# Fetching and multiplying the first strip of each 64-slot unit inside the 128-slot unit ahead of it

## The chip, the core and the metric

The kernel runs on one core of a Trainium2 chip. The metric is the device time of one launch in microseconds; lower is better. The time before is the median of three runs.

## What is computed

The reference is a two-layer decoder trunk on 256 tokens of width 1024. The change lies in its last part, a layer of 8 experts of which each token uses two:

```python
def moe_swiglu(xn, w_router, we_gate, we_up, we_down):
    logits = (xn @ w_router).astype(jnp.float32)
    top_v, top_i = lax.top_k(logits, TOP_K)
    top_w = jax.nn.softmax(top_v, axis=-1)
    gates = jnp.sum(jax.nn.one_hot(top_i, N_EXPERTS, dtype=jnp.float32) * top_w[..., None], axis=-2)
    y = jnp.zeros_like(xn)
    for e in range(N_EXPERTS):
        y = y + gates[..., e:e + 1].astype(xn.dtype) * swiglu(xn, we_gate[e], we_up[e], we_down[e])
    return y
```

All weights are float32; an expert has three matrices of 1024 x 3584, 44 MB in all.

## The kernel before

The experts are ranked by how many tokens they got and worked off as eight units, in turns one of 128 slots (units 0, 2, 4, 6, called wide) and one of 64 slots (units 1, 3, 5, 7, called narrow; `NARROW_UNITS`). A unit gathers its tokens' rows, multiplies them by one expert's weights and scatters the results. Further units, for experts with more tokens than slots, run only when there are any.

**Weights.** A unit has 42 chunks of 1 MB (`FFN_CHUNKS`). They go through a ring of 9 slots in SBUF (`RING`; six of the tile `raw`, two of `spare`, one `late_slot`). SP issues one transfer per chunk in the order in which TensorE uses them (`expert`, L491): gate and up of the first strip of 1024 columns (8 chunks), then twice gate and up of a further strip and four chunks of down (12 chunks each), then a small strip of 512 columns (4 chunks) and the last six chunks of down. `place` (L288) gives the chunk's lap and slot. Before each issue `slot_free` (L427) waits until the slot's former chunk is used: for a narrow unit's chunk until TensorE has multiplied it (`piece_used`), for a wide unit's until it is split (`lo_ready`).

**Wide units** multiply in three terms of a rounded and a remainder part. ScalarE writes the rounded half chunk into `w_hi` (L1596), VectorE the remainder into `w_lo` (L2211). There are six split places of half a chunk, so the splitting runs at most three chunks ahead of TensorE. TensorE (`unit`, L1495) does gate and up of a strip with `e_in_wide`, turns the product of the strip before with `e_turn` (L1317), and multiplies it by down with `e_down`; a chunk has 12 matmuls. Near its end it turns the next unit's gathered rows (`gathered_turned`, L1280).

**Narrow units** multiply the raw chunks in float32, both halves of a chunk into the two 64-partition sides of a bank (`n_in`, `n_down`; 8 matmuls a chunk), the tokens in `x_half`. The product of a strip is a silu on ScalarE (L2067), a multiplication on VectorE (L2982), and four transposes (`n_turn`, L1409). Each engine has its order written out by hand: `narrow_unit` and `unit` on TensorE (L1431, L1495), ScalarE (L2059, L2098) and VectorE (L2975, L3013). Each has waits on counters of what the others have done.

**Rows.** GpSimd gathers the next unit's rows into `xg` (L650), once the slots of that unit are known and the former rows are turned, and scatters a unit's result when it is scaled (L655).

Of the kernel before, what the change touches and what calls it, by code (L numbers as in the profile page):

```python
# [12 lines left out]
P = 128  # L13
# [21 lines left out]
def hybrid_trunk(  # L35
# [45 lines left out]
    with ExitStack() as ctx:  # L81
# [95 lines left out]
        with part:  # L177
# [23 lines left out]
            gslot = sb("gslot", [P, 2], scope=part)  # L201
            rank = sb("rank", [P, 2, NE], scope=part)
# [10 lines left out]
            sb("spare_gap", [P, 168], scope=part)  # L213
# [73 lines left out]

        def place(u, c):  # L288

            return divmod(c - C_MOE + FFN_CHUNKS * u, RING)  # L290
# [21 lines left out]
        def every_other(b):  # L312

            return act_f[:, (b - b % 2) * P + b % 2:(b - b % 2 + 2) * P:2]
# [5 lines left out]
        scaled_before = lambda u: u + wides_before(u)  # L320
        split_chunks = lambda u: FFN_CHUNKS * wides_before(u)
# [57 lines left out]
        def _(sp):  # L379
# [111 lines left out]
            def expert(e, u, c0=C_MOE):  # L491
# [17 lines left out]
                wide(c0, 0)  # L509
                for i in range(WIDE - 1):  # L510
                    c = c0 + WIDE_STEP * i
                    wide(c + 8, i + 1)
                    down_rows(c + 16, 2 * i)
                    down_rows(c + 18, 2 * i + 1)
                c = c0 + SMALL
                for w in small:
                    for j in range(2):
                        src = w[j, here, :, :, (NF - 1) * FC:NF * FC].rearrange("a p k n -> (a p) k n")
                        fetch_expert(u, c, UP, src)
                        c += 1  # L520
                for n, f in enumerate((NF - 3, NF - 2, NF - 1)):
                    down_rows(c + 2 * n, f)

            expert(0, 0)
            sp.wait_ge(sem("order_known"), 1)
            for u in range(1, NE):
                expert(sp.value_load(order_i[0:1, u:u + 1], min_val=0, max_val=NE - 1), u)
# [140 lines left out]
        def _(pe):  # L668
# [606 lines left out]
            def gathered_turned(u):  # L1275
# [3 lines left out]
                for k in range(KD):  # L1279
                    last = pe.transpose(B[k // 4][:, (k % 4) * P:(k % 4) * P + n_rows], xg[0:n_rows, k * P:(k + 1) * P],  # L1280
                                        ident[0:n_rows, 0:n_rows])
                    if k % 4 == 3:
                        last.then_inc(sem("gather_psum"), 1)
# [100 lines left out]
            def n_in(u, c, bank, gathered=None, inside=None):  # L1384

                for k in range(KD):
                    if gathered is not None and k % 4 == 0:
                        pe.wait_ge(sem("gather_ready"), gathered + k // 4 + 1)
# [16 lines left out]
            def n_turn(n, bank, blocks):  # L1405

                pe.wait_ge(sem("act_done"), n + 1)
                for q in range(blocks):
                    last = pe.transpose(B[bank][:, q * P:(q + 1) * P], every_other(q), ident[:, :])  # L1409
# [14 lines left out]
            def next_gate(u):  # L1424

                if u in NARROW_UNITS:
                    n_in(u, C_MOE, 0, gathered=2 * u)
# [3 lines left out]
            def narrow_unit(u, last=False):  # L1431

                n0 = NF + (WIDE + 1) * (u - wides_before(u))
                n_in(u, C_MOE + 4, 1)

                def strip(i, start):
# [5 lines left out]
                    n_down(u, c + 16, n, FB, start, False)  # L1442

                strip(0, True)
# [4 lines left out]
                for i in range(1, WIDE - 1):  # L1449
                    strip(i, False)  # L1450
# [44 lines left out]
            def unit(u, last=False):  # L1495
# [5 lines left out]
                def e_step(i, start):  # L1501
# [5 lines left out]
                    e_in_wide(C_MOE + 12, UP_BANKS, m, inside=lambda: e_turn(n + 1, t + 1, 1))  # L1507
                    e_down(C_MOE + 16, m, t, start)
# [56 lines left out]
        def _(act):  # L1565
# [24 lines left out]
            def split_expert_high(u, p):  # L1590
# [3 lines left out]
                before = u if p - SPLIT_SLOTS >= 2 * C_MOE else last_wide(u) + 1  # L1594
                act.wait_ge(piece_used, p - SPLIT_SLOTS + 1 + 2 * FFN_CHUNKS * before)
# [424 lines left out]
            def e_silu(c, more, n, halves):  # L2020

                act.wait_ge(piece_used, 2 * (c + more))
# [15 lines left out]
            def keep_gate(u):  # L2038

                act.wait_ge(sem("slots_known"), u + 1)  # L2040
                act.activation(gslot[:, :], slot[:, 1:3], ACT.Copy).then_inc(sem("turned"), 1)
# [7 lines left out]
            def rows_out(u):  # L2049

                act.wait_ge(piece_used, 2 * (C_MOE + FFN_CHUNKS * (u + 1)))
# [7 lines left out]
            def narrow_unit(u, last=False):  # L2059

                n0, used = NF + (WIDE + 1) * (u - wides_before(u)), FFN_CHUNKS * u

                def silu(i, c, cols):
                    act.wait_ge(piece_used, 2 * (c + used))
                    if i:
                        act.wait_ge(sem("act_done"), n0 + i)
                    act.activation(silu_g[:, 0:cols], B[0][:, 0:cols], ACT.Silu, scale=gslot[:, 1:2]).then_inc(  # L2067
# [6 lines left out]
                keep_gate(u)  # L2074
                act.wait_ge(sem("turned"), u + 1)
# [1059 lines left out]
```

## Time and profile before

| | us |
|---|---|
| median of three runs | 1369.26 (1369.08 to 1369.85) |
| the profiled execution | 1367.94 |
| its span, from the first to the last instruction | 1366.2 |
| TensorE matmul busy | 1293.7 (95%) |
| VectorE, ScalarE busy | 784.4 (57%), 677.7 (50%) |
| hardware transfers of SP's queue | 429.89 MB, 81.4% of 16 engines' span |
| DMA over the span | 441.53 MB, mean 323 GB/s |

Matmuls are pipelined, so a TensorE that counts as busy is not at its peak, and the share of a whole span is an average over stages with different limits. The experts run from about 490 us to the end. Time to landing is the time from a transfer's issue on SP's queue until its semaphore is raised; a queue with more in it shows a longer one.

### The profile page before, as it was taken

The page shows a single profiled execution, that of the slowest core. Times are in us where ns is not written, and L with a number is a line of the kernel's source. Part 1 is how long each engine was busy: PE and PEld are TensorE (multiplying, and loading weights), DVE is VectorE, ACT ScalarE, POOL GpSimd, SP SyncE. Part 2 cuts the span into 40 slices and gives each one's busy share as a digit, 9 for nine tenths or more (in the row PEclk, how much of TensorE's full clock was granted, in tenths as well). Part 3 has the DMA queues.
Part 4 walks back from the last instruction along what each step waited for, and adds up shares of the span by engine and source line. Part 5 has one row for each costly group of instructions (what it writes and reads, how often), then busy time and mean ns, then how long its engine had stood idle before and what let it go on. Part 6 is the DMA issues. An engine that isn't in the chain of part 4 may idle for free.

```text
span 1366.2 us, 17236 instructions
## 1 busy us (share of the span) xinstructions
PE 1293.7 (95%) x6371; PEld 925.6 (68%) x6371; DVE 784.4 (57%) x1139; ACT 677.7 (50%) x941; POOL 40.9 (3%) x120
## 2 busy tenths in 40 slices
PE   9999999999999999999789999879999888999886
PEld 8998888888887878873248884238885235887222
DVE  6967665544559789960039990009983006996110
ACT  6665644444459658750038771018883006875000
POOL 1000000000001010000000000000000000000100
PEclk9999999999999999999999999999999999999999
DMA  8564475555324599989999999999999999999997
GB/s 305 182 200 145 162 225 185 186 183 183 113 84 173 209 341 372 396 323 407 419 423 422 411 421 379 422 419 420 423 412 386 422 421 420 422 411 386 402 420 293
DMA packets 130689, 441.53 MB, mean 323 GB/s; under 512 B 10690, under 2 KB 23072, under 8 KB 116269
## 3 DMA queue, kind: packets, MB, share of 16 engines
q1 hardware_dynamic: 127084, 429.89, 81.4%
q0 software_dynamic: 3488, 10.54, 2.0%
q8 instruction: 49, 0.80, 0.2%
q14 instruction: 36, 0.29, 0.1%
q10 hardware_dynamic: 32, 0.01, 0.0%
HBM read 434.06 MB, written 8.13 MB: 324 GB/s over the span
## 4 chain that ended last, share of the span: by engine, by line
PE 77%; DMA 18%; ACT 2%; DVE 2%; issue 1%; SPq 1%; POOL 0%; DVEq 0%; ACTq 0%; POOLq 0%
PE bank L670 73%; DMA raw<-in_we_gate_dram 7%; DMA late_slot<-in_we_gate_dram 3%; DMA spare<-in_we_gate_dram 3%; DMA raw<-in_we_down_dram 3%; DMA raw<-in_we_up_dram 1%; PE bank L1317 1%; DVE w_lo L2211 1%; SPq L446 1%; ACT w_hi L1596 1%; PE bank L1015 0%; PE bank L682 0%; ACT xr L1731 0%; PE bank L690 0%; PE bank L1409 0%
## 5 line engine op out<-in xcount | busy, mean ns | idle before, releaser
L670 PE MATMUL bank<-w_hi,xT_hi 128*128 128x512 f32 (+3 forms) x1358 | 461.8, 389 | 11.7 <-DVE w_lo L2211 10.1
L670 PE MATMUL bank<-w_lo,xT_hi 128*128 128x512 f32 (+4 forms) x910 | 348.2, 383 | 0.0
L670 PEld LDWEIGHTS bank<-w_hi,xT_hi 128*128 128x128 f32 x1358 | 257.0, 189 | 66.3 <-issue 14.4
L2211 DVE TENSOR_TENSOR w_lo<-raw,w_hi 128x1024 fp32r<-128x1024 f32 x222 | 260.0, 1218 | 30.0 <-ACT w_hi L1596 26.2
L1596 ACT ACTIVATE w_hi<-raw 128x1024 fp32r<-128x1024 f32 x224 | 231.4, 1060 | 69.7 <-PE bank L670 41.9
L2204 DVE TENSOR_TENSOR w_lo<-raw,w_hi 128x1024 fp32r<-128x1024 f32 (+5 forms) x166 | 178.1, 1102 | 87.4 <-ACT w_hi L1588 86.4
L1588 ACT ACTIVATE w_hi<-raw 128x1024 fp32r<-128x1024 f32 (+5 forms) x164 | 152.7, 971 | 99.7 <-PE bank L670 99.6
L670 PEld LDWEIGHTS bank<-w_lo,xT_hi 128*128 128x128 f32 x910 | 171.7, 189 | 31.1
L2982 DVE SCALAR_TENSOR_TENSOR act_f<-bank,gslot,silu_g 128x512 f32<-128x512 f32 (+1 forms) x16 | 10.9, 684 | 293.0 <-PE bank L670 293.0
L670 PE MATMUL bank<-w_hi,xT_lo 128*128 128x512 f32 (+4 forms) x462 | 173.0, 374 | 0.0
L670 PE MATMUL bank<-raw,x_half 128*64 128x512 f32 (+1 forms) x704 | 140.7, 540 | 19.3 <-DMA raw<-in_we_gate_dram 9.6
L2067 ACT ACTIVATE silu_g<-bank,gslot 128x512 f32<-128x512 f32 (+1 forms) x16 | 10.1, 634 | 254.7 <-PE bank L670 254.7
L670 PE MATMUL bank<-w_hi,aT_hi 128*128 128x512 f32 x320 | 126.4, 395 | 0.0
L670 PE MATMUL bank<-w_lo,aT_hi 128*128 128x512 f32 x320 | 125.7, 393 | 0.0
L670 PE MATMUL bank<-w_hi,aT_lo 128*128 128x512 f32 x320 | 125.2, 391 | 0.0
L670 PEld LDWEIGHTS bank<-raw,x_half 128*64 128x64 f32 x704 | 47.6, 136 | 104.8 <-issue 61.4
L670 PEld LDWEIGHTS bank<-w_hi,xT_lo 128*128 128x128 f32 x462 | 86.7, 188 | 14.1
L2211 DVE TENSOR_TENSOR w_lo<-spare,w_hi 128x1024 fp32r<-128x1024 f32 x72 | 85.1, 1219 | 12.3 <-ACT w_hi L1596 10.6
L1596 ACT ACTIVATE w_hi<-spare 128x1024 fp32r<-128x1024 f32 x72 | 74.4, 1060 | 22.4 <-PE bank L670 10.8
L670 PE MATMUL bank<-raw,a_half 128*64 128x512 f32 x280 | 67.2, 602 | 13.7 <-DMA raw<-in_we_down_dram 13.7
L670 PEld LDWEIGHTS bank<-w_hi,aT_hi 128*128 128x128 f32 x320 | 60.2, 188 | 13.4
L670 PEld LDWEIGHTS bank<-w_hi,aT_lo 128*128 128x128 f32 x320 | 60.1, 188 | 13.4
(435 smaller groups left out, 1166.3 us busy)
## 6 DMA issues: line engine op xcount, KB each, us to landing
raw<-in_we_gate_dram SPq DMA_DIRECT2D x75, 1024.0 KB, 16.6
raw<-in_we_up_dram SPq DMA_DIRECT2D x75, 1024.0 KB, 16.2
raw<-in_we_down_dram SPq DMA_DIRECT2D x75, 1024.0 KB, 15.3
spare<-in_we_up_dram SPq DMA_DIRECT2D x27, 1024.0 KB, 15.8
spare<-in_we_down_dram SPq DMA_DIRECT2D x26, 1024.0 KB, 16.4
spare<-in_we_gate_dram SPq DMA_DIRECT2D x21, 1024.0 KB, 15.1
late_slot<-in_we_gate_dram SPq DMA_DIRECT2D x16, 1024.0 KB, 16.1
raw<-in_w_gate_dram SPq DMA_DIRECT2D x28, 512.0 KB, 4.0
```

The lines of the kernel that those rows point to most:

```text
L446: sp.dma_start(ring_piece(u, c, shape, None), src).then_inc(ring_here(u, c)[0], 16)
L670: return pe.matmul(o, a, b, start=start, stop=stop, skip_group_check=True, **kw)
L1317: last = pe.transpose(B[2][:, q * P:(q + 1) * P], every_other(b), ident[:, :])
L1588: act.activation(split_piece(w_hi, c, shape, half), raw_piece(c, shape, half), ACT.Copy).then_inc(hi_ready, 1)
L1596: act.activation(split_piece(w_hi, c, WROW, half), ring_piece(u, c, WROW, half), ACT.Copy).then_inc(hi_ready, 1)
L2067: act.activation(silu_g[:, 0:cols], B[0][:, 0:cols], ACT.Silu, scale=gslot[:, 1:2]).then_inc(sem("silu_done"), 1)
L2204: dve.tensor_tensor(split_piece(w_lo, c, shape, half), raw_piece(c, shape, half), F(split_piece(w_hi, c, shape, half)), ALU.subtract).then ...
L2211: dve.tensor_tensor(split_piece(w_lo, c, WROW, half), ring_piece(u, c, WROW, half), F(split_piece(w_hi, c, WROW, half)), ALU.subtract).the ...
L2982: dve.scalar_tensor_tensor(out=act_f[:, 0:cols], in0=B[1][:, 0:cols], scalar=gslot[:, 1:2], in1=silu_g[:, 0:cols], op0=ALU.mult, op1=ALU.m ...
```

## The change

The fetch order and TensorE's order of a pair of units change. The first strip (gate and up, 8 chunks) of the narrow unit is fetched after 32 of the wide unit's 42 chunks and multiplied there, into banks 6 and 7. The gathered rows of the narrow unit are turned before the wide unit's second group of down chunks instead of near its end. Its silu, product and transposes go between the wide unit's last steps; the product stands in `y_out` until it is turned. The narrow unit has a tile of gates of its own (`gslot_n`). Counters that were worked out from a unit's number are now worked out from a chunk's place in the new order (`turn_of`, `used_to`). In the narrow unit the second strip's gate and up come first, then the first strip's down.

```diff
+        N_AHEAD, W_BEFORE = 8, 2 * 4 + 2 * 12
+        in_turn = []
+        for u in range(0, NE, 2):
+            in_turn += [(u, i) for i in range(W_BEFORE)] + [(u + 1, i) for i in range(N_AHEAD)]
+            in_turn += [(u, i) for i in range(W_BEFORE, FFN_CHUNKS)] + [(u + 1, i) for i in range(N_AHEAD, FFN_CHUNKS)]
+        in_turn += [(u, i) for u in range(NE, NE + NU_MAX) for i in range(FFN_CHUNKS)]
+        turn_of = {chunk: n for n, chunk in enumerate(in_turn)}
+
         def place(u, c):
 
-            return divmod(c - C_MOE + FFN_CHUNKS * u, RING)
+            return divmod(turn_of[u, c - C_MOE], RING)
+
+        def used_to(u, c):
+
+            return 2 * (C_MOE + turn_of[u, c - C_MOE - 1] + 1)
...
                 lap, s = place(u, c)
                 if lap:
-                    owner, i = divmod(RING * (lap - 1) + s, FFN_CHUNKS)
+                    owner, i = in_turn[RING * (lap - 1) + s]
                     if owner in NARROW_UNITS:
-                        sp.wait_ge(piece_used, 2 * (C_MOE + FFN_CHUNKS * owner + i) + 2)
+                        sp.wait_ge(piece_used, used_to(owner, C_MOE + i + 1))
                     else:
...
+                    ahead()
+                if part in (None, 1):
+                    strips()
+                if part in (None, 2):
+                    end()
+
+            e_of = lambda u: sp.value_load(order_i[0:1, u:u + 1], min_val=0, max_val=NE - 1)
+            for u in range(0, NE, 2):
+                wide_e = e_of(u) if u else 0
+                expert(wide_e, u, 0)
+                expert(wide_e, u, 1)
+                if u == 0:
+                    sp.wait_ge(sem("order_known"), 1)
+                narrow_e = e_of(u + 1)
+                expert(narrow_e, u + 1, 0)
+                expert(wide_e, u, 2)
+                expert(narrow_e, u + 1, 1)
+                expert(narrow_e, u + 1, 2)
 
...
-                def strip(i, start):
+                n0 = first_strip(u)
+                n_in(u, C_MOE + 12, 1)
+                n_down(u, C_MOE + 16, n0, FB, True, False)
+
+                def strip(i):
                     c, n = C_MOE + WIDE_STEP * i, n0 + i
                     pe.wait_ge(sem("silu_done"), n + 1)
                     n_in(u, c + 8, 0)
                     n_turn(n, 2, FB)
                     n_in(u, c + 12, 1)
-                    n_down(u, c + 16, n, FB, start, False)
-
-                strip(0, True)
+                    n_down(u, c + 16, n, FB, False, False)
+
                 if last:
                     turn_rows()
                 else:
                     turn_next(u)
                 for i in range(1, WIDE - 1):
-                    strip(i, False)
+                    strip(i)
...
                     e_in_wide(C_MOE + 12, UP_BANKS, m, inside=lambda: e_turn(n + 1, t + 1, 1))
+                    if i == WIDE - 2 and not last:
+                        pe.wait_ge(sem("esilu_done"), n0 + 2 * WIDE)
+                        gathered_turned(u + 1, (0, 6))
                     e_down(C_MOE + 16, m, t, start)
...
                 pe.wait_ge(sem("esilu_done"), n + 2)
+                if not last:
+                    pe.wait_ge(sem("gather_ready"), 2 * (u + 1) + 2)
+                    n_in(u + 1, C_MOE, 6)
+                    pe.wait_ge(sem("eact_done"), n + 2)
+                    n_in(u + 1, C_MOE + 4, 7)
                 e_in(c, 0, more)
                 e_turn(n, t, 0)
+                if not last:
+                    n_turn(first_strip(u + 1), 6, FB, y_out)
                 e_in(c + 2, 1, more)
                 e_turn(n + 1, t + 1, 1)
 
                 def next_turned():
+                    if not last:
+                        pe.wait_ge(sem("aT_hi_ready"), NF - 2 + first_strip(u + 1) + 1)
                     e_turn_halves(n0 + NF - 1)
-                    if not last:
-                        gathered_turned(u + 1)
...
                     e_high(t0 + 2 * i + 1, 1)
-                    pieces(33, 48, i)
+                    pieces(33, 45, i)
+                    if i == WIDE - 2 and not last:
+                        keep_gate(u + 1, gslot_n)
+                        act.wait_ge(sem("turned"), u + 2)
+                        act.wait_ge(piece_used, used_to(u + 1, C_MOE + 4))
+                        act.wait_ge(sem("eact_done"), n0 + 2 * WIDE)
+                        act.activation(silu_g[:, 0:FC], B[6][:, :], ACT.Silu, scale=gslot_n[:, 1:2]).then_inc(
+                            sem("silu_done"), 1)
+                    pieces(45, 48, i)
                 p, n, t = 2 * SMALL, n0 + NF - 3, t0 + NF - 3
                 pieces(p + 8, p + 9)
                 e_high(t, 0)
-                e_silu(C_MOE + SMALL + 2, more, n + 2, 1)
+                if not last:
+                    act.wait_ge(sem("act_done"), first_strip(u + 1) + 1)
+                e_silu(u, C_MOE + SMALL + 2, n + 2, 1)
+                if not last:
+                    act.wait_ge(sem("aT_psum"), NF + first_strip(u + 1) + 1)
+                    act.activation(a_half[:, 0:FC], B[6][:, :], ACT.Copy).then_inc(sem("aT_hi_ready"), 1)
...
-                        dve.tensor_copy(x_half[:, k, :], B[b][:, :].rearrange("p (k s) -> p k s", k=4)[:, :, 0:HALF_SLOTS]).then_inc(
+                        dve.tensor_copy(x_half[:, k, :], B[6 * b][:, :].rearrange("p (k s) -> p k s", k=4)[:, :, 0:HALF_SLOTS]).then_inc(
...
-                    pieces(37, 48, i)
+                    e_product(u, C_MOE + 16 + WIDE_STEP * i, n0 + 2 * i + 2, 2)
+                    if i == WIDE - 2 and not last:
+                        gathered(u + 1)
+                    pieces(37, 45, i)
+                    if i == WIDE - 2 and not last:
+                        dve.wait_ge(piece_used, used_to(u + 1, C_MOE + 8))
+                        dve.wait_ge(sem("silu_done"), first_strip(u + 1) + 1)
+                        dve.wait_ge(sem("scattered"), scattered_before(u))
+                        dve.scalar_tensor_tensor(out=y_out[:, 0:FC], in0=B[7][:, :], scalar=gslot_n[:, 1:2],
+                                                 in1=silu_g[:, 0:FC], op0=ALU.mult, op1=ALU.mult).then_inc(
+                            sem("act_done"), 1)
+                    pieces(45, 48, i)
```

Left out are the tile `gslot_n`, the counters re-worked with `used_to`, the split of `expert` into its three parts (first strip, middle, end), and the arguments for the banks.

## Rows read from the trace of the kernel before

**Rows 1.** The page's part 4, the chain that ended last, shares by engine.

```profile
PE 77%; DMA 18%; ACT 2%; DVE 2%; issue 1%; SPq 1%; POOL 0%; DVEq 0%; ACTq 0%; POOLq 0%
```

**Rows 2.** Stages: length, busy us by engine, granted clock, DMA busy share, GB/s.

```profile
610.00:620.00 10.00, 10.00 (x48) 3.73 (x48) 0.00 (x0) 2.15 (x4) 1.05 (x1) 1.00 0.64 213
...
650.00:700.00 50.00, 40.77 (x210) 14.72 (x210) 2.52 (x4) 3.81 (x7) 0.36 (x1) 1.00 1.03 422
...
820.00:830.00 10.00, 10.00 (x45) 6.76 (x46) 1.61 (x2) 1.94 (x4) 0.36 (x1) 1.00 0.90 368
830.00:840.00 10.00, 10.00 (x50) 3.32 (x48) 0.00 (x0) 0.69 (x1) 0.83 (x2) 1.00 0.93 326
```

**Rows 3.** The chain of waits in order of time: start us, us, what.

```profile
502.54 0.05 DVE order_i L2848
...
599.38 0.64 PE bank L1280 x8
...
639.70 18.76 DMA raw<-in_we_up_dram
...
703.81 1.07 ACT w_hi L1596
...
706.27 34.50 PE bank L670 x144
...
781.40 21.91 PE bank L670 x96
...
848.98 5.33 PE bank L670 x24
...
920.43 1.06 ACT w_hi L1596
```

**Rows 4.** The gathers into xg: one issue on GpSimd (timeline), landing of all.

```profile
770.73 1.20 POOL L650 DMA_INDIRECT xg<-x_rows,rows_next  x1 [56.08 <-DVE half_rows L2929]
...
DMA to landing us min/median/max: 6.3/7.2/7.9
```

**Rows 5.** Timeline of SP's issues: places 40, 51 (first pair), 50, 51 (second).

```profile
576.41 0.33 SPq L446 DMA_DIRECT2D raw<-in_we_down_dram  x1
...
613.26 0.37 SPq L446 DMA_DIRECT2D spare<-in_we_gate_dram  x1
...
821.89 0.37 SPq L446 DMA_DIRECT2D late_slot<-in_we_gate_dram  x1
...
829.60 0.37 SPq L446 DMA_DIRECT2D raw<-in_we_gate_dram  x1
```

**Rows 6.** Time to landing (last column), first pair, places 40 and 51.

```profile
raw<-in_we_down_dram SPq DMA_DIRECT2D x1, 1024.0 KB, 6.9
...
spare<-in_we_gate_dram SPq DMA_DIRECT2D x1, 1024.0 KB, 6.2
```

**Rows 7.** The same, second pair, places 40, 50 and 51.

```profile
spare<-in_we_down_dram SPq DMA_DIRECT2D x1, 1024.0 KB, 13.2
...
late_slot<-in_we_gate_dram SPq DMA_DIRECT2D x1, 1024.0 KB, 9.2
...
raw<-in_we_gate_dram SPq DMA_DIRECT2D x1, 1024.0 KB, 6.5
```

**Rows 8.** The same, third pair, places 40, 50 and 51.

```profile
raw<-in_we_down_dram SPq DMA_DIRECT2D x1, 1024.0 KB, 13.8
...
raw<-in_we_gate_dram SPq DMA_DIRECT2D x1, 1024.0 KB, 9.9
...
raw<-in_we_gate_dram SPq DMA_DIRECT2D x1, 1024.0 KB, 6.2
```

**Rows 9.** The same, fourth pair, places 40, 50 and 51.

```profile
raw<-in_we_down_dram SPq DMA_DIRECT2D x1, 1024.0 KB, 12.4
...
raw<-in_we_gate_dram SPq DMA_DIRECT2D x1, 1024.0 KB, 8.0
...
spare<-in_we_gate_dram SPq DMA_DIRECT2D x1, 1024.0 KB, 5.5
```

More of the change, by code:

```diff
@@ L201, in hybrid_trunk @@
             gslot = sb("gslot", [P, 2], scope=part)
+            gslot_n = sb("gslot_n", [P, 2], scope=part)
             rank = sb("rank", [P, 2, NE], scope=part)
@@ L212, in hybrid_trunk @@
             half_rows = sb("half_rows", [P, 1], I32, scope=part)
-            sb("spare_gap", [P, 168], scope=part)
+            sb("spare_gap", [P, 160], scope=part)
             spare = sb("spare", [P, 2, CHUNK], scope=part)
@@ L489, in _, with expert @@
                     fetch(c, sizes[c], src)
-            def expert(e, u, c0=C_MOE):
+            def expert(e, u, part=None, c0=C_MOE):
                 gate, up = (w.rearrange("e (j k p) n -> j e p k n", j=4, p=P) for w in (we_gate1, we_up1))
@@ L507, in down_rows @@
                         fetch_expert(u, c + j, DOWN, down[j, here, f:f + 1].rearrange("a b p k n -> (a b p) k n"))
[L509 to L527, printed above, removed]
+                def ahead():
+                    wide(c0, 0)
+                def strips():
+                    for i in range(WIDE - 1):
+                        c = c0 + WIDE_STEP * i
+                        wide(c + 8, i + 1)
+                        down_rows(c + 16, 2 * i)
+                        down_rows(c + 18, 2 * i + 1)
@@ new lines, in end @@
+                def end():
+                    c = c0 + SMALL
+                    for w in small:
+                        for j in range(2):
+                            src = w[j, here, :, :, (NF - 1) * FC:NF * FC].rearrange("a p k n -> (a p) k n")
+                            fetch_expert(u, c, UP, src)
+                            c += 1
+                    for n, f in enumerate((NF - 3, NF - 2, NF - 1)):
+                        down_rows(c + 2 * n, f)
+                if part in (None, 0):
+                    ahead()
@@ L1382, in two_sides, with n_in @@
                 return last
-            def n_in(u, c, bank, gathered=None, inside=None):
+            def n_in(u, c, bank, inside=None):
                 for k in range(KD):
-                    if gathered is not None and k % 4 == 0:
-                        pe.wait_ge(sem("gather_ready"), gathered + k // 4 + 1)
                     raw_landed(u, c + k // 2)
@@ L1426, in next_gate @@
                 if u in NARROW_UNITS:
-                    n_in(u, C_MOE, 0, gathered=2 * u)
+                    n_in(u, C_MOE + 8, 0)
                 else:
@@ L2098, in unit @@
             def unit(u, last=False):
-                more, w = FFN_CHUNKS * u, wides_before(u)
+                w = wides_before(u)
                 n0, t0 = NF * w, (NF - 1) * w
@@ L2131, in unit @@
                     high_part(2 * b, 2, B[(6, 7)[b]]).then_inc(sem("eaT_half_hi"), 1)
-                if not last:
-                    gathered(u + 1)
                 pieces(p + 18, p + 20)
@@ L2975, in narrow_unit @@
             def narrow_unit(u, last=False):
-                n0, used = NF + (WIDE + 1) * (u - wides_before(u)), FFN_CHUNKS * u
+                n0 = first_strip(u)
                 def product(i, c, cols):
-                    dve.wait_ge(piece_used, 2 * (c + used))
+                    dve.wait_ge(piece_used, used_to(u, c))
                     dve.wait_ge(sem("silu_done"), n0 + i + 1)
-                    dve.scalar_tensor_tensor(out=act_f[:, 0:cols], in0=B[1][:, 0:cols], scalar=gslot[:, 1:2],
+                    dve.scalar_tensor_tensor(out=act_f[:, 0:cols], in0=B[1][:, 0:cols], scalar=gslot_n[:, 1:2],
                                              in1=silu_g[:, 0:cols], op0=ALU.mult, op1=ALU.mult).then_inc(
                         sem("act_done"), 1)
-                product(0, C_MOE + 8, FC)
                 if last:
@@ L3013, in unit @@
             def unit(u, last=False):
-                used, w = FFN_CHUNKS * u, wides_before(u)
+                w = wides_before(u)
                 n0, t0 = NF * w, (NF - 1) * w
@@ L3036, in unit @@
                 pieces(14, 21)
-                e_product(C_MOE + 8, used, n0, 2)
+                e_product(u, C_MOE + 8, n0, 2)
                 pieces(21, 24)
@@ L3056, in unit @@
                 pieces(p + 8, p + 13)
-                e_product(C_MOE + SMALL + 4, used, n + 2, 1)
+                e_product(u, C_MOE + SMALL + 4, n + 2, 1)
                 e_low(t + 1, 1)
@@ L3062, in unit @@
                     low_part(2 * b, 2, B[(6, 7)[b]]).then_inc(sem("eaT_half"), 1)
-                pieces(p + 17, p + 18)
-                if not last:
-                    gathered(u + 1)
-                pieces(p + 18, p + 20)
+                pieces(p + 17, p + 20)
                 if last:
```

66 lines of the change are left out of this document (33 added, 33 removed).

## The prediction

> **What bounds the kernel now.** I read the chain of waits first: over the span it is mostly matmuls, and 18% transfers [rows 1]. In order of time it shows a pattern that repeats for each pair of units, one of 128 slots (wide) and one of 64 (narrow). A wide unit is a run of matmuls without a break. From about the twelfth chunk of the narrow unit, at 639.70, weight transfers take over until the first chunk of the next wide unit lands at 703.81; its first matmul follows at 706.27 [rows 3]. Pairs repeat every 216.6 us (703.81 to 920.43).
>
> Rates say why. 96 matmuls of a wide unit take 21.91 us; a chunk of 1 MB has 12, so 2.74 us. In a narrow unit 24 take 5.33, a chunk has 8: 1.78 us [rows 3]. Transfers bring 422 GB/s when their queue is full [rows 2]: 1.0486 MB in 2.49 us. So TensorE is slower than the transfers in a wide unit, faster in a narrow one. A pair costs TensorE 42 x 2.74 + 42 x 1.78 = 190 us plus some 10 of transposes and starting, and the transfers 84 x 2.49 = 209 plus gather, scatter and whatever they stand idle. The transfers are therefore the bound of a pair, and a gain can only come from their idle time.
>
> The stages show where they idle: 0.64 busy share at 610 to 620, 0.90 and 0.93 at 820 to 840, against 1.03 in the narrow part [rows 2]. This is the crossing from wide to narrow. A wide chunk's ring slot is free once ScalarE and VectorE have split it, up to three chunks ahead of TensorE; a narrow one's only when TensorE has used it. At the crossing TensorE works off the last three split chunks (36 matmuls, 8.2 us) and no slot comes free: SP's issues stand from 821.89 to 829.60, g = 7.7 us, the same at all four crossings [rows 5]. By then the lead of the transfers has filled the ring, and little is left in the queue: the time from issue to landing, 13.2 us at place 40 of the pair (places count its chunks in fetch order, from 0), is down to 9.2 at place 50 [rows 7].
>
> **The cost, by landings.** Place 50 lands at 821.89 + 9.2 = 831.1, place 51, which finds an empty queue, at 829.60 + 6.5 = 836.1. Of these 5.0 us the chunk itself needs 2.49: idle 2.5 us [rows 5, 7]. The same with g = 7.7 for the next pairs: 7.7 + 6.2 - 9.9 - 2.5 = 1.5 us and 7.7 + 5.5 - 8.0 - 2.5 = 2.7 us [rows 8, 9]. In the first pair TensorE has been the bound since its start: place 40 lands at 576.41 + 6.9 = 583.3, place 51 at 613.26 + 6.2 = 619.5 [rows 5, 6], 36.2 us for 11 chunks that need 27.4: idle 8.8 us.
>
> **What the change does to it.** Places 0 to 31 stay; 32 to 39 are now the narrow unit's first gate and up strip, 40 to 49 the wide unit's last ten chunks, 50 to 83 the rest.
>
> *The gap moves.* It now lies before place 41 is issued (its slot is that of place 32, the first narrow chunk) and again before 59. The 8.2 us of matmuls in front are the same, so I take g = 7.7 again. The transfers stay busy if the last issue before the gap has a time to landing of at least g + 6.2 - 2.49 = 11.4 us (6.2 being the empty queue's [rows 6]). At place 40 it is 13.2, 13.8 and 12.4 in pairs two to four [rows 7 to 9]: no idle time, with 1.0 to 2.4 us to spare. In the first pair it is 6.9: idle 4.5 us.
>
> *The second gap.* Call the issue of 41 time 0. It lands at 13.2 + 2.5 - 7.7 = 8.0, and each place after it 2.49 later. The narrow chunks free slots every 1.78, so the queue fills. TensorE ends the eight at 12.5 and does ten wide chunks and about 2 us of transposes till 42; the split that frees place 49's slot comes at about 36. So 58 is issued at 36 and lands at 8.0 + 17 x 2.49 = 50.3: 14 us, above 11.4. In the first pair 41 is issued at 584.1 and lands at 590.3, 58 at 632.6, issued at about 620: 12.5, above it too.
>
> *First pair.* From 590.3 on landings follow every 2.49, so place 51 lands at 615.2 instead of 619.5: 4.3 us gained.
>
> *New waits.* On ScalarE the narrow silu stands behind the split of place 42's first half. Place 42 lands at 8.0 + 2.5 = 10.5, split by 11.6, silu by 12.7; VectorE's product needs TensorE's eighth chunk (12.5) and ends near 14. TensorE asks for it only after the small gate's two chunks, at 18.5: 4 us to spare. Each of these passes is at most a 128x1024 one, 1.07 us [rows 3]. Queued behind these waits, on ScalarE and on VectorE, are the splits of places 42 and 43, wanted at 19 and 21 and ready by 18. The gathered rows are wanted earlier: at 786.9 (781.40 plus 24 of the 96 matmuls) instead of at 815. Their gather is issued at 770.73 and takes 7.2 us [rows 3, 4]: 9.0 us to spare. SP loads the expert numbers as often as before; its wait for the order of experts comes ten issues earlier, at about 553 (eight wide chunks before 576.41), 50 us after the order is made at 502.54 [rows 3, 5]. POOL's queue keeps its order.
>
> *TensorE's work.* Same products; the 0.64 us of transposes of the gathered rows [rows 3] move ahead; one set of four transposes moves. A pair's 200 us stay under 213, so this is covered by the transfers; were the cover gone, it would cost what it adds, under 1 us a pair. Waits of other engines are re-counted, not added: nothing.
>
> **Sum.** 4.3 + 2.5 + 1.5 + 2.7 = 11.0 us. The profiled execution took 1367.94 us, 1.3 below the median of the runs, 1369.26; I take the sum off the median: 1358.3 us.
>
> Bounds of the unknown. The empty-queue landing is 5.5 to 6.5 in the rows [rows 6 to 9], the gap is not shown in its new place. From below: g stays at least 7.1 (8.2 of matmuls, 1.8 of the first chunk, less the 2.5 to 3 that a split comes early), which changes only the first pair, by 0.6. Counting bytes instead of landings, the stretch 820 to 840 lacks 54 and 96 GB/s of 422 over 10 us each, 3.5 us instead of 2.5 [rows 2], because the scatter runs there too; 1 us more a pair gives 15 at most. From above: g = 10, if three splits' time is lost to VectorE's x_half copies and the product, costs 2.3 in the first pair, 0.5, 0 and 1.3 in the others, a gain of 6.9. I take 11.0, since 7.7 is the gap at every crossing of the rows.
>
> On the price of a lone transfer the trace shows 5.5 to 6.5 us from issue to landing [rows 6 to 9]. The Trainium skill, page "DMA: Bandwidth & Descriptors", section "Anatomy of one DMA — SWDGE (gpsimd) path", fits 2.0 us plus the bytes over 436 GB/s, an estimate of 4.4 us for a chunk. With that figure the first pair's new idle would be 2.7 instead of 4.5, and the sum 12.8. The rows have the same kind of transfer, so they decide.
>
> **Rivals.**
>
> *The gap is longer in its new place.* For it: splits of the wide unit's last chunks, x_half copies and the product share VectorE there. Against: VectorE has slack around each. At g = 10 to 11 the gain is 7 to 4 us: 1362 to 1365, say 1363.
>
> *The transfers are full already.* If 820 to 840 is a limit of the memory and not idleness, the change moves nothing: 1369.3. For it: a busy share above 0.9 there. Against: 422 GB/s for 50 us in the same pair [rows 2], and a landing gap of 5.0 us behind issues that stood. The Trainium skill, page "DMA: Bandwidth & Descriptors", section "Where 436 GB/s comes from", has the memory side bind at about 358 GB/s for transfers from HBM to SBUF; by it the 368 of that stretch would be all there is. The trace disagrees, 422 for long stretches, so this keeps little chance.
>
> *Slower: TensorE stands for the gathered rows.* The wait now lies in the middle of the wide unit. With a wait of w the gap grows by w, the first pair idles 4.5 + w and the others w - 1.8, w - 2.4 and w - 1.0; the gain is 11.0 - (4w - 5.2) = 16.2 - 4w. It turns at w = 4, and at 4.7 the kernel is 2.7 us slower, 1372; at 6 it is 1377. The gather would have to take 16.2 + 4.7 = 20.9 us. Against: 6.3 to 7.9 us in all seven, under a full weight queue [rows 4]. For: nothing but that a weight chunk behind a full queue takes above 13 [rows 8].
>
> **Numbers.** Forecast 0.68, longer gap 0.18, full already 0.07, slower 0.07. The forecast's own range is 1354 to 1361; with the longer gap it reaches 1364, which leaves out the last two rivals: 1354 to 1364. A measurement of this kernel tells 0.2% (2.7 us) from no change: faster 0.86, same 0.07, slower 0.07.
>
> **What would show it.** In the profile after, right: SP stands about 7.7 us before place 41 and 59; the busy share at the crossings of pairs two to four is 1.0 and the first pair still shows one dip, near 585; pairs repeat every 213 to 215 us; the transfer-bound part of a narrow unit is shorter. Wrong: a time to landing under 7 us after either gap in pairs two to four, TensorE waiting for gathered rows, for the narrow product or for a split inside a wide unit, or a landing rate under 415 GB/s with full queues.

## The result, and the profile after

The changed kernel takes 1357.16 us, the median of 4 runs (1355.81 to 1358.27), against 1369.55 for the kernel before in the same comparison: a ratio of 0.9909, 95% interval 0.9892 to 0.9926. That is 12.4 us faster; 11.0 us were forecast, to 1358.3. A later comparison of the same two kernels gave 9.6 us (below), so the size is known to some 1.5 us either way. The profiled execution took 1356.84 us, with a span of 1355.1 against 1366.2: 11.1 us between the two traces, and these are what I now take apart.

The chain that ended last, shares by engine (the page of the changed kernel; [rows 1] before):

```profile
PE 78%; DMA 17%; DVE 2%; ACT 2%; issue 1%; SPq 0%; POOL 0%; DVEq 0%; ACTq 0%; POOLq 0%
```

A share of the span hardly shows a gain of one per cent. The chain in order of time does (changed kernel: start us, us, what; [rows 3] before):

```profile
638.94 15.07 DMA raw<-in_we_up_dram
...
699.00 1.06 ACT w_hi L1643
...
913.67 1.06 ACT w_hi L1643
...
1128.27 1.06 ACT w_hi L1643
```

Line 704 is the matmul line that was line 670. The transfer-bound part of the first narrow unit still begins at 639 and is 4 us shorter: 638.94 to 699.00, 60.1 us, where it was 639.70 to 703.81, 64.1 us. Pairs now repeat every 214.7 us (699.00 to 913.67, then 214.6), before 216.6 and 215.9.

The stages (changed kernel: length, busy us by engine, granted clock, DMA busy share, GB/s; [rows 2] before):

```profile
570.00:580.00 10.00, 10.00 (x48) 8.20 (x47) 6.22 (x8) 2.99 (x3) 0.00 (x0) 1.00 0.94 340
580.00:590.00 10.00, 10.00 (x47) 3.87 (x47) 2.36 (x2) 3.05 (x4) 0.00 (x0) 1.00 0.77 263
...
610.00:620.00 10.00, 10.00 (x47) 8.29 (x46) 9.58 (x13) 6.43 (x8) 0.00 (x0) 1.00 1.02 419
650.00:700.00 50.00, 40.56 (x210) 14.61 (x206) 2.52 (x4) 4.80 (x9) 0.00 (x0) 1.00 1.02 421
820.00:830.00 10.00, 10.00 (x47) 8.30 (x46) 9.70 (x11) 7.07 (x9) 0.00 (x0) 1.00 1.01 418
830.00:840.00 10.00, 10.00 (x47) 6.05 (x47) 0.84 (x4) 1.27 (x2) 1.01 (x1) 1.00 1.03 421
```

The three stages that were thin are full: 610 to 620 went from 213 to 419 GB/s, 820 to 840 from 368 and 326 to 418 and 421. In the first pair a dip has come up at 580 to 590, as forecast. SP's issues show both gaps (timeline of SP's queue, changed kernel: places 40 and 41, then 58 and 59 of the first pair, then 40 and 41, 58 and 59 of the second; [rows 5] before):

```profile
576.25 0.38 SPq L460 DMA_DIRECT2D raw<-in_we_gate_dram  x1
...
583.46 0.38 SPq L460 DMA_DIRECT2D raw<-in_we_gate_dram  x1
...
619.22 0.34 SPq L460 DMA_DIRECT2D raw<-in_we_down_dram  x1
...
627.05 0.34 SPq L460 DMA_DIRECT2D raw<-in_we_down_dram  x1
...
787.34 0.37 SPq L460 DMA_DIRECT2D spare<-in_we_gate_dram  x1
...
794.55 0.37 SPq L460 DMA_DIRECT2D late_slot<-in_we_gate_dram  x1
...
830.18 1.31 SPq L460 DMA_DIRECT2D spare<-in_we_down_dram  x1
...
838.01 0.34 SPq L460 DMA_DIRECT2D late_slot<-in_we_down_dram  x1
```

And the times to landing of the first six of these issues (last column; [rows 6, 7] before):

```profile
raw<-in_we_gate_dram SPq DMA_DIRECT2D x1, 1024.0 KB, 7.6
...
raw<-in_we_gate_dram SPq DMA_DIRECT2D x1, 1024.0 KB, 5.5
...
raw<-in_we_down_dram SPq DMA_DIRECT2D x1, 1024.0 KB, 13.1
...
raw<-in_we_down_dram SPq DMA_DIRECT2D x1, 1024.0 KB, 8.6
...
spare<-in_we_gate_dram SPq DMA_DIRECT2D x1, 1024.0 KB, 14.1
...
late_slot<-in_we_gate_dram SPq DMA_DIRECT2D x1, 1024.0 KB, 9.5
```

SP still stands for 7.2 us before place 41 and 7.8 before place 59, where it stood for 7.7 once. In the second pair nothing is lost by it: place 40 lands at 787.34 + 14.1 = 801.4 and place 41 at 794.55 + 9.5 = 804.05, 2.6 us apart, and a chunk needs 2.49. The standing is doubled and the idling has nearly gone.

By pairs, worked out from the first landing of each wide unit in the chains of the two traces (us; the first column is when the order of experts is known, the last pair reaches to the end of the span):

```
          order    pair 1  pair 2  pair 3  pair 4 + tail   span
before    502.54   201.27  216.62  215.94  229.83          1366.2
after     501.68   197.32  214.67  214.60  226.83          1355.1
gain        0.86     3.95    1.95    1.34    3.00            11.1
forecast             4.3     2.5     1.5     2.7             11.0
```

### The profile page after: what moved, and what is told of

It reads as the page before. It is cut to its first block, busy times and chain, and to the rows that moved or that the text cites. A ratio compares the mean times of both kernels' runs of the same rounds, so it can differ in the third digit from the quotient of the medians.

```text
span 1355.1 us, 17232 instructions
## 1 busy us (share of the span) xinstructions
PE 1291.0 (95%) x6371; PEld 924.8 (68%) x6371; DVE 783.9 (58%) x1139; ACT 675.4 (50%) x941; POOL 39.3 (3%) x120
## 3 DMA queue, kind: packets, MB, share of 16 engines
q0 software_dynamic: 3488, 10.54, 2.0%
## 4 chain that ended last, share of the span: by engine, by line
PE 78%; DMA 17%; DVE 2%; ACT 2%; issue 1%; SPq 0%; POOL 0%; DVEq 0%; ACTq 0%; POOLq 0%
PE bank L704 74%; DMA raw<-in_we_gate_dram 9%; DMA spare<-in_we_gate_dram 3%; DMA raw<-in_we_down_dram 3%; DMA raw<-in_we_up_dram 2%; PE bank L1351 1%; DVE w_lo L2266 1%; SPq L460 0%; PE bank L1049 0%; PE bank L716 0%; ACT xr L1778 0%; ACT w_hi L1643 0%; PE bank L724 0%; ACT w_hi L1630 0%; PE bank L1151 0%
## 5 line engine op out<-in xcount | busy, mean ns | idle before, releaser
L3037 DVE SCALAR_TENSOR_TENSOR act_f<-bank,gslot_n,silu_g 128x512 f32<-128x512 f32 (+1 forms) x12 | 7.9, 662 | 232.0 <-PE bank L704 232.0
L2114 ACT ACTIVATE silu_g<-bank,gslot_n 128x512 f32<-128x512 f32 (+1 forms) x12 | 7.4, 616 | 200.2 <-PE bank L704 177.0
L704 PEld LDWEIGHTS bank<-w_hi,aT_lo 128*128 128x128 f32 x320 | 60.1, 188 | 13.8
```

Of the source, the lines that this page charges most:

```text
L704: return pe.matmul(o, a, b, start=start, stop=stop, skip_group_check=True, **kw)
L3037: dve.scalar_tensor_tensor(out=act_f[:, 0:cols], in0=B[1][:, 0:cols], scalar=gslot_n[:, 1:2], in1=silu_g[:, 0:cols], op0=ALU.mult, op1=ALU ...
```

## The experiments

The theory: the gain is idle time of the transfers behind SP's standing issues, and whether a gap idles them is decided by how much is still queued when it begins. Rivals: the crossing got shorter on TensorE, since the gathered rows are turned and copied out of its way; or it is TensorE's time at large that counts, wherever in the pair it is spent. The kernels ran beside the kernel before: 1367.64 us (21 runs) for the first four, 1367.62 (17 runs) for the next four, 1370.79 (11 runs) for the last. Differences by pair are taken from the traces, against the two rows of the table above; a trace is one execution, and the fourth pair has the end of the kernel in it, of which the stretch behind the last landing alone varies between 10.1 and 13.3 us in these traces.

**The early turning alone.** The kernel before, with only the turning and copying of the narrow unit's gathered rows put where the change puts it.

```diff
+                    if i == WIDE - 2 and not last:
+                        pe.wait_ge(sem("esilu_done"), n0 + 2 * WIDE)
+                        gathered_turned(u + 1, (0, 6))
                     e_down(C_MOE + 16, m, t, start)
...
                     e_turn_halves(n0 + NF - 1)
-                    if not last:
-                        gathered_turned(u + 1)
...
                     e_product(C_MOE + 16, used + WIDE_STEP * i, n0 + 2 * i + 2, 2)
+                    if i == WIDE - 2 and not last:
+                        gathered(u + 1)
```

> The kernel before, with one part of the change alone: the gathered rows of a narrow unit are turned and copied into x_half ahead of the wide unit's second group of down chunks; the narrow strip itself stays where it was. Queue theory (the gain is transfer time that stood idle behind the gap in SP's issues): 0, 1369.5 us, at most 1 us either way. Rival that the gain is TensorE's shorter crossing (turning and copying no longer stand at the unit's end): most of the 12 us, 1360 or below.

Measured: 1368.5 us (10 runs), ratio 1.0019 (1.0000 to 1.0038). The stage of the first crossing stayed thin (stages of this kernel):

```profile
610.00:620.00 10.00, 10.00 (x49) 3.43 (x50) 0.00 (x0) 2.15 (x4) 1.23 (x2) 1.00 0.71 233
```

So this part of the change gives nothing by itself: the rival of a shorter crossing falls. It also costs next to nothing, as the prediction had it.

**A longer gap before the change.** 26 transposes of the identity (about 3 us) ahead of the first narrow chunk at the crossing, into a bank that nothing reads before it is written anew; they add work and change no result.

```diff
                 if u in NARROW_UNITS:
+                    keep_busy(26, 3)
                     n_in(u, C_MOE, 0, gathered=2 * u)
```

> The kernel before with 26 transposes of the identity (about 3.05 us of TensorE, into a bank that nobody reads then) ahead of the first narrow chunk of each narrow unit, so the gap in SP's issues at the crossing grows from 7.7 to some 10.7 us. Queue theory: there is no backlog to spare, so four times 3.05, +12 us, 1381.5. Rival that TensorE is the bound: the same +12. Rival that the transfers are full there: 0, 1369.5.

Measured: 1375.36 us (6 runs), ratio 1.0050 (1.0032 to 1.0068): some 7 to 8 us, not 12. By pairs 1.8, 1.3, 2.8 and 1.9. The first transposes, from the timeline of TensorE in this kernel:

```profile
611.69 3.00 PE L690 MATMUL bank<-ident 128*128 128x128 f32 x26
```

Places 50 and 51 of its second pair, issue and then time to landing (SP's timeline, and the table of transfers):

```profile
824.10 0.37 SPq L446 DMA_DIRECT2D late_slot<-in_we_gate_dram  x1
...
834.64 0.37 SPq L446 DMA_DIRECT2D raw<-in_we_gate_dram  x1
```

```profile
late_slot<-in_we_gate_dram SPq DMA_DIRECT2D x1, 1024.0 KB, 9.3
...
raw<-in_we_gate_dram SPq DMA_DIRECT2D x1, 1024.0 KB, 5.0
```

The gap has grown as meant, from 7.7 to 10.5 us, but place 51 now needs 5.0 us to land and not 6.5: the landings are 10.54 + 5.0 - 9.3 = 6.2 us apart instead of 5.0, so 1.2 of the 2.8 us count. GpSimd's scatter moved at the same time. In the kernel before (GpSimd's timeline, and the table of transfers) it starts with that chunk, 0.04 us after its issue at 829.60, and takes 7.1 us (7.0 to 8.8 at the four crossings):

```profile
829.64 1.00 POOL L655 DMA_INDIRECT y_rows<-y_out,rows_now  x1 [57.71 <-ACT y_out L2145]
...
y_rows<-y_out,rows_now POOLq DMA_INDIRECT x1, 7.1
```

In this kernel it runs in the empty time and takes 3.2 (3.2 to 3.3 at all four):

```profile
831.85 1.00 POOL L655 DMA_INDIRECT y_rows<-y_out,rows_now  x1 [57.70 <-ACT y_out L2146]
...
y_rows<-y_out,rows_now POOLq DMA_INDIRECT x1, 3.2
```

The sign fits the theory. My price of one to one does not. The reading that fits the rows is that another queue with something to move uses part of the idle time; it was not tried apart from the longer gap.

**A longer gap after the change.** The same 26 transposes, ahead of the narrow chunks in their new place.

```diff
                     pe.wait_ge(sem("gather_ready"), 2 * (u + 1) + 2)
+                    keep_busy(26, 3)
                     n_in(u + 1, C_MOE, 6)
```

> The changed kernel with the same 26 transposes ahead of the first narrow chunk inside each wide unit. Queue theory, from the backlogs of the trace after at place 40 (7.6, 14.1, 11.8 and 11.2 us against 10.7 needed for a gap of 7.2): +3 in the first pair, 0 in the second, 2 to 3 in the third and fourth, together +8 us, 1365 (1363.5 to 1367). Rival that TensorE is the bound: +12, 1369.4. Rival that the transfers are full: 0, 1357.

Measured: 1365.12 us (10 runs), ratio 0.9968 (0.9952 to 0.9985). That is 7.3 us above the next kernel, which ran beside it and has the same added work elsewhere, and 8.3 us by the traces against the changed kernel; 8 were expected. By pairs 2.5, -0.1, 2.8 and 3.0, of which 1.2 lie behind the last landing. The second pair has the largest backlog at place 40 (14.1 us) and pays nothing for 3 us of TensorE's time. Two stages of this kernel, the dip of the first pair and the crossing of the second:

```profile
580.00:590.00 10.00, 10.00 (x61) 5.78 (x61) 2.36 (x2) 2.00 (x2) 0.00 (x0) 1.00 0.48 163
...
830.00:840.00 10.00, 10.00 (x46) 8.26 (x46) 5.91 (x9) 3.70 (x5) 0.00 (x0) 1.00 1.03 419
```

**The same work where TensorE waits anyway.** The changed kernel, the 26 transposes ahead of the small strip of each narrow unit (with a wait that keeps the bank safe).

```diff
                 pe.wait_ge(sem("silu_done"), n + 1)
+                pe.wait_ge(*((sem("onehotT_ready"), 1) if last else (sem("slot_copied"), u + 2)))
+                keep_busy(26, 3)
                 n_in_small(u, c, 0)
```

> The changed kernel with the same 26 transposes ahead of the small strip of each narrow unit, where TensorE waits for transfers anyway. Queue theory: 0 to +1 us, 1357.5, as the same added work lies where the queue is full. Rival that TensorE is the bound: +12, 1369.4.

Measured: 1357.78 us (4 runs), ratio 0.9926 (0.9903 to 0.9949): nothing, beside 1358.03 of the changed kernel in the next comparison. The chain of this kernel walks through the transposes and comes back to the transfers:

```profile
674.12 2.99 PE bank L724 x26
```

Together with the run before it, this places the bound: 3 us of TensorE ahead of a free slot cost 8 us over four pairs, 3 us behind full transfers cost none.

**A ring of 8 slots.** One line, in the kernel before and in the changed one; the queue can hold 1 MB less.

```diff
-RING = 9
+RING = 8
```

> The kernel before with a ring of 8 slots instead of 9. Queue theory: the gap comes one place earlier and finds one chunk (2.5 us) less in the queue, so about +2.5 us a pair, +10, 1379.5 us. Rival that the gain came from TensorE's order: the ring moves both kernels alike.

> The changed kernel with a ring of 8 slots. Queue theory: +2.5 in the first pair, 0 in the second (backlog 14.1 less 2.5, against 10.7), about 2 in the third and the fourth, +6 to +7 us, 1363.5; the distance between the two kernels grows from 12 to about 16 us. Rival that the gain came from TensorE's order: the distance stays 12.

Measured: the kernel before with 8 slots 1379.89 us (4 runs), ratio 1.0083 (1.0059 to 1.0106), 12.3 us slower; the changed one 1363.34 us (10 runs), ratio 0.9971 (0.9957 to 0.9984), 5.3 us above the changed kernel. So the change is worth 16.5 us with 8 slots, where 16 were expected, and 9.6 with 9 in the same comparison, where 12 were. The crossing of the second pair, first with the old order, then with the new one (stages of each):

```profile
820.00:830.00 10.00, 10.00 (x45) 8.20 (x44) 4.56 (x7) 2.12 (x2) 0.00 (x0) 1.00 0.97 387
830.00:840.00 10.00, 10.00 (x49) 3.35 (x49) 0.00 (x0) 2.16 (x4) 1.01 (x1) 1.00 0.65 214
```

```profile
830.00:840.00 10.00, 10.00 (x45) 8.03 (x43) 4.88 (x8) 2.54 (x4) 0.00 (x0) 1.00 1.03 421
```

No work of any engine is changed here, only the depth of the queue. By pairs the kernel before loses 2.7, 2.5, 3.6 and 6.7 us in its profiled execution, which was the slowest of the four. In the second, third and fourth pair the landings fall behind at the crossing, between places 48 and 60; 2.7 of the 6.7 lie behind the last landing. In the first pair the loss is there by place 40, ahead of the crossing, and is not explained by the backlog at the gap. The changed kernel loses 2.6, 0.9, 0.9 and 2.3: the second pair, for which 0 was expected, pays too. With this limit it is the plainest evidence for the backlog: where less is queued when SP stands, the transfers idle.

**The changed kernel again**, as a measure of the others.

> The changed kernel unaltered, beside the next one: 1357.2 us, within 1.5 of its first runs.

Measured: 1358.03 us (6 runs), ratio 0.9927 (0.9909 to 0.9945). Its pairs are 197.25, 215.37, 214.75 and 226.16 us.

**The first gap taken away.** From the changed kernel: the fetch order stays, but TensorE multiplies the narrow strip after the second of the four down chunks ahead of it, so that narrow slots come free before the split slots run out.

```diff
+                    def first_of_next():
+                        pe.wait_ge(sem("gather_ready"), 2 * (u + 1) + 2)
+                        n_in(u + 1, C_MOE, 6)
+                        pe.wait_ge(sem("eact_done"), n0 + 2 * WIDE)
+                        n_in(u + 1, C_MOE + 4, 7)
+
-                    e_down(C_MOE + 16, m, t, start)
+                    e_down(C_MOE + 16, m, t, start, inside=first_of_next if i == WIDE - 2 and not last else None)
```

> The changed kernel with the fetch order kept, but TensorE multiplies the narrow unit's first strip after the second of the four down chunks in front of it instead of after the fourth. Two wide chunks that are split already stand back, so slots come free every 1.8 us and the gap before place 41 falls from 7.2 to about 2 us. Queue theory: the idle time left in the trace after (2.6 and 0.8 us in the first pair, 1.2 in the third, some 0.5 in the fourth) goes, 3 to 5 us, 1353 (1351.5 to 1355). Rival that TensorE is the bound, or that no idle time is left: 0, 1357.

Measured: 1357.63 us (6 runs), ratio 0.9924 (0.9907 to 0.9942): the same as the changed kernel, so the forecast of 1353 missed. The profiled execution was the fastest of the six, with a span of 1352.9. Its stages:

```profile
580.00:590.00 10.00, 10.00 (x47) 3.26 (x44) 2.36 (x2) 2.01 (x2) 0.00 (x0) 1.00 1.05 402
...
620.00:630.00 10.00, 10.00 (x46) 5.47 (x46) 0.00 (x0) 1.27 (x2) 1.04 (x1) 1.00 0.91 351
630.00:640.00 10.00, 10.00 (x50) 3.40 (x48) 0.75 (x1) 0.69 (x1) 0.18 (x1) 1.00 0.98 377
```

The dip at 580 to 590 is gone, as meant, and a smaller one has come up at the second gap: the time to landing at place 58 of the first pair is 10.0 us, where the second run of the changed kernel had 12.9, and the landings behind it are 4.6 and 3.7 us apart instead of 3.4 and 2.5. In that pair, what was won at one gap lowered the backlog at the next. The profiled execution is 3 us below the median of the six, so its smaller gains in the other pairs cannot be set against the median.

**Both gaps.** The kernel above, with the gate chunks of the narrow unit's second strip also multiplied ahead of the wide unit's last four down chunks.

```diff
                     e_turn_halves(n0 + NF - 1)
+                    if not last:
+                        n_in(u + 1, C_MOE + 8, 0)
...
-                if u in NARROW_UNITS:
-                    n_in(u, C_MOE + 8, 0)
-                else:
+                if u not in NARROW_UNITS:
                     e_in_wide(C_MOE, GATE_BANKS, split_chunks(u), gathered=2 * u)
```

> The kernel of mid_strip with the same cure at the second crossing: TensorE multiplies the gate chunks of the narrow unit's second strip after the second of the wide unit's last six down chunks, so the gap before place 59, where the first pair's idle time went in mid_strip (backlog 10.0 us there instead of 12.9), falls from 7.8 to some 3 us. Queue theory: 3 us less in the first pair (about 194 from the order of experts to the next wide unit's first landing, instead of 196.8), up to 1 in the others, 1354 us (1352 to 1356). If idle time only moves on to the next place where slots come free slowly, 196.8 stays, and 1357.

Measured: 1362.46 us (6 runs), ratio 0.9939 (0.9921 to 0.9958); 1354 was expected. The kernel before took 1370.79 us in this comparison, and the interval overlaps that of the changed kernel (0.9909 to 0.9945). So it is not shown that this kernel is slower than the changed one; it is shown that the expected gain did not come.

The edit did not shorten the standing. SP's issues of places 57 and 58 in the first pair, and their times to landing:

```profile
617.86 0.37 SPq L467 DMA_DIRECT2D raw<-in_we_up_dram  x1
...
627.37 0.35 SPq L467 DMA_DIRECT2D raw<-in_we_down_dram  x1
```

```profile
raw<-in_we_up_dram SPq DMA_DIRECT2D x1, 1024.0 KB, 9.9
...
raw<-in_we_down_dram SPq DMA_DIRECT2D x1, 1024.0 KB, 4.8
```

SP stands 9.5 us here and 11.5 to 12.0 in the other pairs, where 3 were meant and 7.8 stood before place 59. Place 58 goes into the slot of place 49, the wide unit's last chunk. TensorE now does four narrow chunks ahead of the last four wide ones, so that chunk is split later, and the narrow slots that are free early are of no use: SP issues in order. With the standing as it is, the theory holds: 9.5 + 4.8 - 9.9 - 2.5 = 1.9 us idle in the first pair, where the landings are 4.4 us apart; 11.8 + 5.0 - 14.4 - 2.5, none, in the second, where they are 2.5 apart.

TensorE's timeline shows two new waits in the second pair (idle time and its releaser in brackets):

```profile
830.43 1.94 PE L711 MATMUL bank<-raw,x_half 128*64 128x512 f32 x8 [0.51 <-DMA raw<-in_we_gate_dram]
...
849.83 2.37 PE L711 MATMUL bank<-raw,x_half 128*64 128x512 f32 x10 [1.36 <-ACT y_out L2209]
```

The chunks that it pulls ahead have not landed yet, and the scaling of the wide unit's result on ScalarE (`y_out`) is no longer covered by them. These waits cost nothing in that pair: it took 214.67 us, against 215.37 in the second run of the changed kernel. Of the 5.6 us between these two traces 4.9 lie in the fourth pair, 2.8 of them behind the last landing; why is open. No version of mine beats the changed kernel.

## Why the prediction was right, point by point

**What bounds the kernel.** That a gain could only come from idle time of the transfers holds: 3 us of added TensorE work is free where they are full and costs where a slot waits for it, and one slot less in the ring costs at the crossings of the second to fourth pair.

**The gap.** I took 7.7 us from the old crossing with 7.1 as the lowest. It is 7.2 before place 41 in all four pairs and 7.8 before place 59. The rival of a longer gap, 10 us, did not come about; made by hand (10.0 us, from 576.27 to 586.32 in the first pair) it cost 2.5, -0.1, 2.8 and 3.0 us by pairs, where the working at g = 10 had 2.3, 0.5, 0 and 1.3: too cheap in the last two, whose backlog I had too large. (At g = 11 that working leaves a gain of 3.0 us, not 4.)

**The first pair.** Idle 4.5 us was forecast for the new gap; by landings, 583.46 + 5.5 - 576.25 - 7.6 = 5.1 us between places 40 and 41 makes 2.6. The gap was 0.5 shorter, the backlog 0.7 larger, and the lone transfer took 5.5 us where I had taken 6.2. Yet the pair gained 3.95 us and not 6: the sum counted one landing step behind a gap, and the next step is long as well (3.42 us between places 41 and 42). After the second gap 3.4 us pass between places 58 and 59, though the backlog of 13.1 us is above my bound of 11.4. That is not idle time, as the stage shows (changed kernel; the second line is the stretch behind the second gap of the second pair):

```profile
627.00:635.70 8.70, 8.70 (x42) 2.87 (x40) 0.00 (x0) 0.69 (x1) 1.18 (x2) 1.00 1.03 430
...
838.00:845.40 7.40, 7.40 (x37) 2.45 (x35) 0.00 (x0) 0.69 (x1) 1.01 (x1) 1.00 1.02 421
```

The transfers are full, and the scatter moves among them, 627.13 to 635.44 in the first pair. Before the change it lay in the idle time of the crossing; now it takes its share of a full queue. The sum put it at nothing.

On that lone transfer the rows now show 5.5 us in the changed kernel and 5.0 in the two kernels with the longer gap. The 5.5 to 6.5 us that I read as the price of an empty queue were no lone transfers: at all four crossings of the kernel before, a scatter starts less than 0.1 us behind that chunk's issue. The Trainium skill, page "DMA: Bandwidth & Descriptors", section "Anatomy of one DMA — SWDGE (gpsimd) path", has a fit for transfers that GpSimd issues, which makes an estimate of 4.4 us for a chunk; these chunks are issued by SP, and the runs come nearer to that estimate than the rows before did, and stay above it.

**The other pairs.** Forecast gains of 2.5, 1.5 and 2.7 were 1.95, 1.34 and 3.0. The backlog at place 40 was 14.1, 11.8 and 11.2 us where 13.2, 13.8 and 12.4 were taken from the order before: the third and fourth pairs begin their gap with less, and places 40 and 41 land 3.7 and 2.6 us apart, 2.6 in the second pair. So about 1.2 us are lost there in the third pair, where nothing was forecast. The bound of 11.4 is a soft one: in the second run of the changed kernel the backlog is 11.6 and the step 2.6 us, though the pair is no shorter (214.75 us).

That these gains came so near is in part luck, and the second pair shows why. Before, places 50 to 52 land 5.06 and 3.27 us apart, 3.3 us more than two chunks need; the sum counted the first step alone, 2.5. After, nothing is lost there, but places 56 and 57 land 3.7 us apart while the scatter moves in a full queue (second stage above), 1.2 us more than a chunk needs. 3.3 - 1.2 = 2.1 is what remains, and 1.95 was measured: two terms that the sum left out, of opposite sign. The scatter's bytes, 0.32 MB on GpSimd's queue, make 0.8 of the 1.2 us at 421 GB/s; the rest is open.

The remaining 0.86 us of the 11.1 lies ahead of the experts, where the change does nothing: the order of experts is known 0.86 us earlier in that execution (501.68 against 502.54). In the second run of the changed kernel it is known at 502.57. The pairs alone gained 10.2 us by the first trace and 10.1 by the second, against 11.0 forecast.

**The transfers are full already.** This rival falls with the stages: 418 to 421 GB/s at the crossing that had 326 and 368. The Trainium skill, page "DMA: Bandwidth & Descriptors", section "Where 436 GB/s comes from", has the memory side bind at about 358 GB/s for these transfers, and in the same note names a measured 425 GB/s. The trace disagrees with the first and is near the second, with 421 over 50 us and now at the crossings as well.

**The new waits.** Timeline of ScalarE, VectorE and TensorE in the second pair of the changed kernel:

```profile
801.46 2.00 ACT L1643 ACTIVATE w_hi<-spare 128x1024 fp32r<-128x1024 f32 x2 [16.03 <-DMA spare<-in_we_gate_dram]
...
807.75 0.69 ACT L2171 ACTIVATE silu_g<-bank,gslot_n 128x512 f32<-128x512 f32 x1
...
808.80 0.75 DVE L3111 SCALAR_TENSOR_TENSOR y_out<-bank,gslot_n,silu_g 128x512 f32<-128x512 f32 x1
...
792.44 1.94 PE L704 MATMUL bank<-late_slot,x_half 128*64 128x512 f32 x8
...
812.38 0.64 PE L1441 MATMUL bank<-ident,y_out 128*128 128x128 f32 x4
```

The silu stands behind the splits of places 40 to 42, as forecast, and the product ends at 809.55. TensorE asks for it at 812.38: 2.8 us to spare, where 4 was forecast. The first narrow matmul follows the one ahead of it without a wait, so the gathered rows were there and the rival that ends slower stood on a wait that never came: the gathers landed in 7.1 to 7.7 us, in the kernel before in 6.7 to 7.9 (the 6.3 of [rows 4] is a read of earlier results into the same tile, and the gather of the second pair took 7.7 us, not the median of 7.2).

## What to carry to other kernels

Where one in-order queue feeds a ring, ask of each spell in which no slot comes free how much is still in flight when it begins; the spell costs only what that backlog does not cover. Moving work so that the backlog is full when the spell comes can be worth more than shortening it, and a second spell later is then free too. Price the idle time by landings over several steps, not the first alone, and look for what other queues do in it: what they move there is hidden, and comes back as a cost when the idle time is gone. Before TensorE's order is changed to shorten a spell, work out for each slot when it comes free and in which order the queue asks for it: a slot that is free early is of no use while the queue stands for the one before it.

## What the runs showed that I had not expected

A transfer that shares its start with a scatter lands later than one that does not: 5.5 to 6.5 us at the four crossings of the kernel before, 4.9 to 5.1 in that kernel with the longer gap, and the scatter itself takes 7.0 to 8.8 instead of 3.2 to 3.3 us. The standing ahead of the second was longer too, so the scatter's share of the difference is not measured by itself.

In unit 7 of the changed kernel eight matmuls took 2.95 us instead of 1.94, at a granted clock of 0.66 over 10 us, a mean between the two levels, 1.2 and 2.4 GHz. TensorE had waited 2.49 us for a chunk just before. The line of the timeline and that of the stage:

```profile
1290.19 2.95 PE L704 MATMUL bank<-late_slot,x_half 128*64 128x512 f32 x8 [2.49 <-DMA late_slot<-in_we_gate_dram]
```

```profile
1290.00:1300.00 10.00, 8.14 (x26) 2.41 (x28) 0.00 (x0) 0.00 (x0) 0.00 (x0) 0.66 1.03 422
```

The transfers were full there (1.03, 422 GB/s), so it cost nothing. The wait follows eight reads of earlier results on GpSimd's queue (its timeline, the first two):

```profile
1278.56 1.16 POOL L698 DMA_DIRECT2D xg<-y_rows  x2 [0.27 <-issue]
```

That they delayed the chunk was not tried. Nor were a ring of more than 9 slots, or moving the strip in some of the pairs only.
